# Attention on values: both heads of a pair in one visit of TensorE, alternating between the output halves

## The reference

```python
out = jnp.einsum('bnhgqk,bnkhd->bnqhgd', probs.astype(v.dtype), vb)     # A
out = jnp.einsum('bnhqk,bnkhd->bnqhd', probs.astype(v.dtype), vb)       # B
return jnp.einsum('bhqs,bshd->bqhd', p.astype(v.dtype), v)              # C
merged = (gates[:, :, 0] * (ya @ w_br_a) + gates[:, :, 1] * (yb @ w_br_b)
          + gates[:, :, 2] * (yc @ w_br_c))
```

## Time and profile before

| what | value |
|---|---|
| median of three runs | 1634.05 us (1633.14 to 1634.21) |
| span of the profiled execution (first to last instruction) | 1634.0 us |
| time around that span | no own time is recorded for the profiled execution; its span is 0.05 us off the median |
| TensorE (PE) busy | 1577.9 us, 97% |
| DVE busy | 1026.3 us, 63% |
| ACT busy | 714.4 us, 44% |
| records of the value products (L687) | 544 |

### The profile page before, as it was taken

The page is one execution under the profiler, slowest core; times in us unless marked ns, Lnnn a source line. Parts: engine busy times, 40 slices in busy tenths (PEclk is TensorE's granted clock), DMA queues, the critical chain, the costliest instruction groups (busy, mean ns, idle before and its releaser), DMA issues.

```text
span 1634.0 us, 22891 instructions
## 1 busy us (share of the span) xinstructions
PE 1577.9 (97%) x7216; PEld 1267.1 (78%) x7216; DVE 1026.3 (63%) x1821; ACT 714.4 (44%) x1212; POOL 60.9 (4%) x48
## 2 busy tenths in 40 slices
PE   7479999999999999999999999999999999999998
PEld 5357777778888888888878777777888888888886
DVE  7167766555568773577568676655465877447764
ACT  5255555333344432243447555543334443224344
POOL 3000000000020000000110000000002000000001
PEclk9789999999999999999999999999999999999999
DMA  8451221223333323332353212222233332333222
GB/s 178 49 142 52 61 62 54 65 65 90 110 91 93 99 84 98 109 97 83 87 142 91 66 53 65 58 59 65 84 110 88 100 95 86 91 116 94 88 82 89
DMA packets 266400, 142.68 MB, mean 87 GB/s; under 512 B 20396, under 2 KB 263348, under 8 KB 266296
## 3 DMA queue, kind: packets, MB, share of 16 engines
q1 hardware_dynamic: 264656, 137.97, 29.8%
q0 software_dynamic: 1040, 2.63, 1.5%
q10 hardware_dynamic: 600, 0.81, 0.2%
HBM read 136.67 MB, written 4.72 MB: 87 GB/s over the span
## 4 chain that ended last, share of the span: by engine, by line
PE 92%; another core or an unknown queue 3%; DVE 2%; issue 1%; DMA 1%; ACT 1%; SPq 0%; ACTq 0%; DVEq 0%
PE dense L628 28%; PE dense L629 26%; PE dense L630 26%; PE branch L687 5%; PE turned L673 2%; PE scores L659 1%; PE scores L660 1%; PE scores L663 1%; PE dense L833 0%; DVE hg L1114 0%; DMA raw<-in_w_in 0%; DVE wlo L1094 0%; DMA gains<-in_gains 0%; DVE h L1107 0%
## 5 line engine op out<-in xcount | busy, mean ns | idle before, releaser
L628 PE MATMUL dense<-hg,whi 128*128 128x512 f32 x1376 | 552.6, 402 | 38.4 <-DVE wlo L1094 34.2
L630 PE MATMUL dense<-hg,wlo 128*128 128x512 f32 x1376 | 537.5, 391 | 0.0
L629 PE MATMUL dense<-hg,whi 128*128 128x512 f32 x1376 | 537.5, 391 | 0.0
L847 ACT ACTIVATE whi<-raw 128x1024 fp32r<-128x1024 f32 (+3 forms) x277 | 269.4, 972 | 524.6 <-PE dense L630 484.6
L1094 DVE TENSOR_TENSOR wlo<-raw,whi 128x1024 fp32r<-128x1024 f32 (+3 forms) x277 | 310.0, 1119 | 204.9 <-ACT whi L847 203.5
L628 PEld LDWEIGHTS dense<-hg,whi 128*128 128x128 f32 x1376 | 258.8, 188 | 112.2 <-issue 56.4
L630 PEld LDWEIGHTS dense<-hg,wlo 128*128 128x128 f32 x1376 | 258.8, 188 | 55.9
L629 PEld LDWEIGHTS dense<-hg,whi 128*128 128x128 f32 x1376 | 259.1, 188 | 50.0 <-issue 0.7
L628 PE MATMUL dense<-act,whi 128*128 128x512 f32 x608 | 239.6, 394 | 0.7 <-DVE wlo L1094 0.7
L629 PE MATMUL dense<-act,whi 128*128 128x512 f32 x608 | 236.8, 389 | 0.0
L630 PE MATMUL dense<-act,wlo 128*128 128x512 f32 x608 | 236.8, 389 | 0.0
(11 more groups left out here) (132 smaller groups left out, 1322.2 us busy)
## 6 DMA issues: line engine op xcount, KB each, us to landing
raw<-in_w_up SPq DMA_DIRECT2D x88, 512.0 KB, 3.8
raw<-in_w_gate SPq DMA_DIRECT2D x48, 512.0 KB, 3.7
raw<-in_w_in SPq DMA_DIRECT2D x28, 512.0 KB, 3.9
raw<-in_w_down SPq DMA_DIRECT2D x32, 384.0 KB, 3.4
raw<-in_w_down SPq DMA_DIRECT2D x32, 320.0 KB, 3.1
raw<-in_w_out SPq DMA_DIRECT2D x16, 512.0 KB, 3.8
raw<-in_w_br_a SPq DMA_DIRECT2D x16, 256.0 KB, 3.9
raw<-in_w_in SPq DMA_DIRECT2D x12, 256.0 KB, 4.9
```

What stands on the lines that cost most here:

```text
L628: mm(out, a, xhi, start=start, stop=False)
L629: mm(out, a, xlo, start=False, stop=False)
L630: return mm(out, b, xhi, start=False, stop=stop)
L847: fn(whi[:, s, 0:cols], raw[:, r, 0:cols], ACT.Copy).then_inc(w_hi.sem, 1)
```

## The change

`step_pv`, which did one head in every round, becomes `both_pv`, which does both heads of a pair and tile in every second (odd) round. For each tile of keys it issues the matmul of head 0 and then that of head 1, so the output alternates between partitions 0 to 63 and 64 to 127. It is called in round i with step i - 5, waits until the turned probabilities of step i - 4 are there, and reads both `probT` tiles. The semaphore `pv` is still raised once for each head, after that head's last matmul. Nothing else is changed: ACT's copy still waits for `pv.at(l, i - 2)`.

```diff
-            def step_pv(l, i):
-                p, t, s = STEPS[i]
-                pe.wait_ge(p_t.sem, p_t.at(l, i))
-                if (t, s) == (0, 0):
+            def both_pv(l, i):
+                p, t, _ = STEPS[i]
+                pe.wait_ge(p_t.sem, p_t.at(l, i + 1))
+                if t == 0:
                     pe.wait_ge(y_lo.sem, y_lo.at(l, p - 1))
                 vc = 0 if p < A_PAIRS else p - 3
-                if (t, s) == (0, 0):
+                if t == 0:
                     pe.wait_ge(v_done.sem, v_done.at(l, vc))
                 nk = width(i) // P
                 for j in range(nk):
-                    last = mm(bank_y[s * HD:(s + 1) * HD, t * P:(t + 1) * P],
-                              v[:, vc, t + 1 - nk + j, s * HD:(s + 1) * HD],
-                              probT[i % 2][:, j * P:(j + 1) * P], start=j == 0, stop=j == nk - 1)
-                last.then_inc(pv.sem, 1)
+                    for s in range(2):
+                        last = mm(bank_y[s * HD:(s + 1) * HD, t * P:(t + 1) * P],
+                                  v[:, vc, t + 1 - nk + j, s * HD:(s + 1) * HD],
+                                  probT[s][:, j * P:(j + 1) * P], start=j == 0, stop=j == nk - 1)
+                        if j == nk - 1:
+                            last.then_inc(pv.sem, 1)
 
             def attention_step(l, i):
                 if i < NSTEP:
                     step_scores(l, i)
                 if TURN <= i < NSTEP + TURN:
                     step_turn(l, i - TURN)
-                if PV <= i:
-                    step_pv(l, i - PV)
+                if PV < i and (i - PV) % 2 == 1:
+                    both_pv(l, i - PV - 1)
```

## The result

The changed kernel takes 1585.37 us (median of 4 runs, 1583.98 to 1585.49) against 1634.13 before: a ratio of 0.970, 95% interval 0.9686 to 0.9713, so 3.0% faster. The forecast was 1592 with a range down to 1587. The direction was right, and so were the two sources of the gain, fewer visits and overlap of the two halves.

What follows compares the result with a forecast made beforehand. TensorE's own instruction order was taken to set the time. From the profiled span, 1634.0 - 21.8 (fewer visits) - 22.9 (overlap) + 2.5 (weight loads) = 1591.8, so 1592 us, range 1587 to 1614.

Steps and rivals of the forecast that it cites:

- (a): Value products on TensorE: 64 fewer visits at 0.34 us each save 21.8 us, bounds 9 and 21.8.
- (b): Alternating halves inside a visit: records of the two halves overlap, 208 paces of 0.11 saved, 22.9 us, bounds 0 and 22.9.
- The prediction's own sign of being wrong: Visit of 8 records: time to the next dense matmul being neither 0.69 us (overlap) nor 1.02 (no overlap).
- (c): Weight loads of the products: with overlap they must come faster, costing 0 to 19 us; 2.5 taken.
- (d): ACT's copy of even steps starts 0.6 to 1.2 us later, but slack covers it: 0 taken; 19 us if not.
- (e): Other engines once PE is faster: DVE at 84% in the attention stretch; 0 taken, upper bound 5 us.
- any wait of PE in this stretch: Attention stretch: PE showing waits there would mean the prediction is wrong.
- the base: Profiled execution's span of 1634.0 us, 0.05 us from the runs' median, so the forecast was said to carry over.
- No overlap (1612): Rival for the products: the halves don't overlap, only the fewer visits save time; 1612 us, 32%.
- A wait at each change of half (1648): Rival for the products: each of 208 changes of half exposes 0.17 us, 35.4 us in all; 1648 us, 4%.

Runs made afterwards that it cites:

- e4: Changed kernel with both heads of a visit writing the same half of the output partitions, every matmul overwriting (output not the reference's); 1613.33 us.
- e2: Against e3: each visit with more than one key tile cut in two, one part ahead of the transposes, one behind; 1596.53 us.
- e5: Changed kernel with fewer visits: some take two query tiles at once, 24 visits fewer; 1576.96 us.
- e1: Changed kernel with all matmuls of head 0 before all of head 1 inside each visit; 1591.7 us.
- e7: Changed kernel with the heads' matmuls alternating two and two instead of one and one; 1585.53 us.
- e3: Changed kernel with both heads' products issued ahead of the round's transposes instead of behind them; 1579.74 us.

## Why the prediction came out as it did

**What bounds the kernel, and the price of a visit (a): right.** 0.34 us a visit was read from starts alone. The trace after has the same three pieces, e4 gives 21.3 us for the 64 visits, e2 0.35 us each by starts and 0.37 by the medians, e5 0.33 each.

**The overlap (b): right in kind, mis-sized.** This is the term that failed. The prediction said "a matmul is two records on the same half, so a visit runs A A B B A A B B", and made the second A the first that could run beside a B: 2 nk + 1 paces. In the trace both records of head 1's matmul run beside those of head 0's, from the visit's first moment, and a visit takes 2 nk paces. The saving is 272 paces, 29.9 us, not 208 and 22.9; e4 puts it at 28 to 28.5. What failed is the strict order of starts across the halves: e1 at nk = 2 and e7 contradict it even if the order is counted in whole matmuls. Whether the queue holds the two records of a float32 matmul as one entry, or as two of which several can be passed, no run tells apart. The upper bound was drawn from the strict order, so the range inherited the error and had no room below 1587. The prediction's own sign of being wrong came: 0.58 us for a visit of 8 records is neither its 0.69 nor its 1.02.

**The weight loads (c): the 2.5 us weren't there.** Eight loads in a visit of 0.58 us keep up with eight records: they come in pairs, one for each half. The Trainium skill (TensorE: Matmul & The Clock Gate, Part 3) has loads overlap running matmuls only across row groups; here both halves use all rows, and the four loads in the first 0.11 us of a visit do overlap. The same part says that matmuls start and end in program order; at nk = 2 in e1 two matmuls start at once in the order A A B B, and the visit is over in 0.60 us, which can't be if the first B waits for the second A. The measurement decides in both.

**Waits (d) and other engines (e): right to within some 1 us.** In the changed kernel PE waits for ACT's copy once in each layer, at the transposes of the first round that has a visit (111.50 and 867.96 us). The second of the two:

```profile
867.07 0.49 ACT L930 ACTIVATE prob<-prob,nmx 128x256 f32<-128x256 f32 x1
...
867.28 0.28 PE L660 MATMUL scores<-act 128*128 128x256 f32 x1
...
867.56 0.25 ACT L937 ACTIVATE probT<-turned 128x128 f32<-128x128 f32 x1
...
867.96 0.41 PE L673 MATMUL turned<-consts,prob 128*128 128x128 f32 x2 [0.40 <-ACT probT L937]
```

The transposes stand 0.68 us behind the second scores matmul instead of 0.12, so some 1.1 us are lost in the two layers. ACT's copy started late behind an exponential, not behind the product, so it belongs to (e): DVE and ACT had less time for each round. The prediction had named any wait of PE in this stretch as a sign of being wrong; this one is small beside the error of (b).

**Sum.** 1634.0 - 21.8 - 29.9 = 1582.3; with 1.1 us of waits 1583.4, and the profiled span is 1583.6. One more error stood in the base. Every run for which both are recorded takes some 1.8 us more than its span (the profiled run of the changed kernel 1585.38 against 1583.6). The span of 1634.0 before therefore stands for a run of an estimated 1635.8, 1.7 above the median, and that it lay 0.05 us from the median was luck of that execution. The forecast was 8.2 us too high in span (7.0 from (b), 2.5 from (c), less 1.1 of waits, makes 8.4), and the base hid 1.7 of it: 6.6 us against the median.

**The rivals.** No overlap (1612) is what e4 measured, with both heads on one half. A wait at each change of half (1648) is excluded: the changes cost nothing.

## What to carry to other kernels

Here small matmuls that fill half of the array's columns cost a whole pace for each record unless they alternate between the halves; alternate at each matmul, or at least after every second one. Collect them in few visits, since each visit costs a fixed 0.34 us here whatever is in it. Where some other matmul changes the array's set-up anyway, put the visit next to it. When a trace shows two records for one instruction, do not build an order of starts on them, or a bound of the range, before a run shows what can pass what.

## What the runs showed of the hardware that wasn't expected

Queueing is one deep past a blocked matmul: with two for one half at the head, the other half starts at once (0.60 us for 8 records); with three or four it starts only when all but one of the others have started (1.07 and 1.51 us). Whether that is a waiting place for each half or a look-ahead of a fixed number of entries, and whether an entry is a matmul or a record, isn't settled by these orders. Going from the 4-row form straight to the 64-column form takes 0.32 us, no more than going from it to transposes (0.31), and saves 0.19 us a round (e3). And leaving the 64-column form is some 0.05 us cheaper into a transpose than into a dense matmul; why was not tried.
